# Cached keys and values of a decoder layer: each quad of DMAs split between SyncE's and GpSimd's queues

## What is computed

```python
# fox heads: pages of 128 keys, 8 pages for each of 8 sequences
k_all = concat([cache_fox_k[page_table], ka]); v_all = concat([cache_fox_v[page_table], va])
s = q @ k_all.T * scale + (cum_q - cum_k)        # cum: running sum of log-forget values
oa = softmax(s masked causally) @ v_all
# dilated heads: windows (128, step 1), (512, step 4), (2048, step 16) over a cache of 1024 keys
s = q @ kx[idx].T * scale + bias[distance bucket]
ob = sum over the three patterns of softmax(s) @ vx[idx], weighted by their log-sum-exp
heads = concat([oa, ob]); x = x + gate * (heads @ w_out)
```

## Time and profile before

| | |
|---|---|
| runs | 2654.03 us median of 3 (2649.22 to 2661.18) |
| profiled execution | 2655.89 us; its span from the first to the last instruction 2654.2 us |
| TensorE products / VectorE / ScalarE / GpSimd busy | 94% / 43% / 32% / 2% of the span |
| mean granted TensorE clock | 0.967 |
| DMA | 613.6 MB moved; SyncE's queue ("hardware_dynamic") 603.8 MB, GpSimd's ("software_dynamic") 7.9 MB |
| chain of work that ended last | TensorE 86%, DMA 7%, VectorE 2%, SyncE's issuing 2% |

### The profile page before, as it was taken

The page is one execution under the profiler, slowest core; times in us unless marked ns, Lnnn a source line. Parts: engine busy times, 40 slices in busy tenths (PEclk is TensorE's granted clock), DMA queues, the critical chain, the costliest instruction groups (busy, mean ns, idle before and its releaser), DMA issues.

```text
span 2654.2 us, 50741 instructions
## 1 busy us (share of the span) xinstructions
PE 2487.4 (94%) x20807; PEld 2302.4 (87%) x20807; DVE 1150.1 (43%) x1726; ACT 852.7 (32%) x1060; POOL 44.3 (2%) x92
## 2 busy tenths in 40 slices
PE   5789999999999999899998867798999999999999
PEld 2589999999999999899996334597999999999999
DVE  0433444343443345666641112355444444454444
ACT  1423232333232334534431112335333333333332
POOL 0040000000000000000000000000000000000000
PEclk8799999999999999999998878898999999999999
DMA  9687777677777744344558999853454544454444
GB/s 373 259 318 296 275 309 285 263 280 301 286 282 280 303 162 164 125 158 153 181 198 311 346 347 397 330 173 125 160 172 160 171 160 164 161 169 171 158 160 160
DMA packets 105445, 613.63 MB, mean 231 GB/s; under 512 B 16008, under 2 KB 16288, under 8 KB 55648
## 3 DMA queue, kind: packets, MB, share of 16 engines
q1 hardware_dynamic: 101728, 603.81, 62.1%
q0 software_dynamic: 3584, 7.88, 1.0%
HBM read 604.36 MB, written 7.28 MB: 230 GB/s over the span
## 4 chain that ended last, share of the span: by engine, by line
PE 86%; DMA 7%; DVE 2%; SPq 2%; issue 1%; ACT 1%; ACTq 0%; DVEq 0%
PE banks L592 26%; PE banks L591 26%; PE banks L593 25%; PE banks L619 4%; DMA adax<-in_w_ada_dram 3%; SPq L468 1%; PE banks L886 1%; DMA kv_h<-in_vpool_dram 1%; PE banks L843 1%; DMA kv_raw<-in_wink_dram 1%; DMA kv_z<-in_wink_dram 1%; DVE w_lo L1151 1%; SPq L459 1%; PE banks L705 1%; PE banks L532 1%
## 5 line engine op out<-in xcount | busy, mean ns | idle before, releaser
L591 PE MATMUL banks<-h_hi,w_hi 128*128 128x288 f32 x3792 | 1125.5, 297 | 35.0 <-DVE h_lo L1183 19.2
L592 PE MATMUL banks<-h_lo,w_hi 128*128 128x288 f32 x3792 | 1124.0, 296 | 0.0
L593 PE MATMUL banks<-h_hi,w_lo 128*128 128x288 f32 x3792 | 1122.5, 296 | 0.0
L1151 DVE TENSOR_TENSOR w_lo<-raw,w_hi 128x1024 fp32r<-128x1024 f32 (+2 forms) x666 | 763.6, 1188 | 476.4 <-ACT w_hi L923 469.7
L923 ACT ACTIVATE w_hi<-raw 128x1024 fp32r<-128x1024 f32 (+2 forms) x666 | 671.4, 1031 | 710.0 <-PE banks L593 563.4
L591 PEld LDWEIGHTS banks<-h_hi,w_hi 128*128 128x128 f32 x3792 | 718.1, 189 | 47.6 <-issue 41.4
L592 PEld LDWEIGHTS banks<-h_lo,w_hi 128*128 128x128 f32 x3792 | 718.2, 189 | 0.8
L593 PEld LDWEIGHTS banks<-h_hi,w_lo 128*128 128x128 f32 x3792 | 717.5, 189 | 0.0
L591 PE MATMUL banks<-g_hi,w_hi 128*128 128x288 f32 x1376 | 407.9, 296 | 0.0
L592 PE MATMUL banks<-g_lo,w_hi 128*128 128x288 f32 x1376 | 406.8, 296 | 0.0
L593 PE MATMUL banks<-g_hi,w_lo 128*128 128x288 f32 x1376 | 406.6, 296 | 0.0
(11 more groups left out here) (189 smaller groups left out, 1082.3 us busy)
## 6 DMA issues: line engine op xcount, KB each, us to landing
raw<-in_w_dram SPq DMA_DIRECT2D x172, 1024.0 KB, 4.9
adaw<-in_w_ada_dram SPq DMA_DIRECT2D x56, 1024.0 KB, 6.9
adaw_b<-in_w_ada_dram SPq DMA_DIRECT2D x56, 1024.0 KB, 11.3
raw<-in_w_dram SPq DMA_DIRECT2D x64, 896.0 KB, 4.6
raw<-in_w_in_dram SPq DMA_DIRECT2D x49, 1024.0 KB, 4.9
adax<-in_w_ada_dram SPq DMA_DIRECT2D x32, 1024.0 KB, 8.6
raw<-in_w_dram SPq DMA_DIRECT2D x32, 960.0 KB, 4.8
raw<-in_w_out_dram SPq DMA_DIRECT2D x16, 1024.0 KB, 5.0
```

Source lines behind the costliest of these rows:

```text
L591: pe.matmul(bank[:, 0:T], hi, m_hi[:, k, :], start=k == 0, stop=False)
L592: pe.matmul(bank[:, 0:T], hi, m_lo[:, k, :], start=False, stop=False)
L593: last = pe.matmul(bank[:, 0:T], lo, m_hi[:, k, :], start=False, stop=k == nk - 1)
L1151: dve.tensor_tensor(w_lo[:, r, a:b], raw[:, r, a:b], w_hi[:, r, a:b].bitcast(F32), ALU.subtract).then_inc(S["lo_ready"], 1)
```

## The change

The loop's body becomes a function that issues a part `js` of a quad's four transfers on a given engine, with its waits, its page numbers and a semaphore of its own kind (`kv` or `kw`). SyncE issues sequences 0 and 1 of each quad, GpSimd sequences 2 and 3. GpSimd does so after its last store of line 513; the eight toe loads stand in its order between quads 29 and 30. TensorE waits for both kinds, 32 counts each. The waits for free buffers are the same on both queues.

```diff
+        def half_quad(eng, m, js, mark):
+            kind = 0 if m < quad0[1] else 1
+            n = KIND[kind]["n"]
+            g, v, p = (m - quad0[kind]) // (2 * n), (m - quad0[kind]) // n % 2, (m - quad0[kind]) % n
+            if m == 0:
+                eng.wait_ge(S["head_ready"], 16)
+                eng.wait_ge(S["lf_ready"], 1)
+            if m == 1:
+                eng.wait_ge(S["lo_ready"], 2 * out.n0)
+            if m == 2:
+                eng.wait_ge(S["w_used"], 2 * out.n0)
+            if kind == 1 and (m - 1) % RING == 2:
+                eng.wait_ge(S["heads_stored"], 4 * 16)
+                eng.wait_ge(S["p_s"], HEADS)
+            if kind == 0:
+                pg = [eng.value_load(pages[0:1, (GB * g + j) * PAGES + p:(GB * g + j) * PAGES + p + 1],
+                                     min_val=0, max_val=POOL - 1) for j in js]
+            if m > RING:
+                eng.wait_ge(S["kv_used"], m + 1)
+            for a, j in enumerate(js):
...
+                eng.dma_start(kv(m, j), src.rearrange("a p n -> p (a n)"))\
+                   .then_inc(S[f"{mark}_landed{(m - 1) % RING}" if m else f"{mark}_first_landed"], 16)
...
             sp.wait_ge(S["ld_pages"], 16)
             for m in range(QUADS):
...
+                half_quad(sp, m, (0, 1), "kv")
...
             pool.dma_start(lf_out, lf[:, :]).then_inc(S["heads_stored"], 16)
+            for m in range(quad0[1] - 2):
+                half_quad(pool, m, (2, 3), "kw")
             pool.wait_ge(S["p_s"], HEADS)
             for a in range(0, P, REVS):
                 pool.dma_start(toe[a:a + REVS, :, :],
...
+            for m in range(quad0[1] - 2, QUADS):
+                half_quad(pool, m, (2, 3), "kw")
...
                 def landed(m):
-                    if m:
-                        pe.wait_ge(S[f"kv_landed{(m - 1) % RING}"], 64 * ((m - 1) // RING + 1))
-                    else:
-                        pe.wait_ge(S["kv_first_landed"], 64)
+                    for mark in ("kv", "kw"):
+                        if m:
+                            pe.wait_ge(S[f"{mark}_landed{(m - 1) % RING}"], 32 * ((m - 1) // RING + 1))
+                        else:
+                            pe.wait_ge(S[f"{mark}_first_landed"], 32)
```

More of the change, by code:

```diff
@@ L285, in decoder_layer @@
             hy_ready head_ready lft_sum lft_ready ncum_sum ncum_ready p_s p_max p_exp p_scaled p_v p_vcopy
-            p_t p_tcopy p_o p_high p_low vn_sum vn_ready kv_landed0 kv_landed1 kv_landed2 kv_first_landed
+            p_t p_tcopy p_o p_high p_low vn_sum vn_ready kv_landed0 kv_landed1 kv_landed2 kv_first_landed kw_landed0 kw_landed1 kw_landed2 kw_first_landed
             kv_used qbd_ready nm_ready exp_ready r_ready pt_sum pt_ready os_ready ot_ready oh_ready ol_ready"""
@@ L360, in splits @@
                 split(after_norm[r], j, 0, (q,))
+        def half_quad(eng, m, js, mark):
[18 more added lines that the diff above has]
+            for a, j in enumerate(js):
+                if kind == 0:
+                    src = (vpool if v else kpool)[bass.ds(pg[a], 1), :, :]
+                else:
+                    src = (winv if v else wink)[GB * g + j:GB * g + j + 1, p, :, :]
+                eng.dma_start(kv(m, j), src.rearrange("a p n -> p (a n)"))\
+                   .then_inc(S[f"{mark}_landed{(m - 1) % RING}" if m else f"{mark}_first_landed"], 16)
         def own_rows(c):
@@ L443, in _ @@
             for m in range(QUADS):
[L444 to L465, removed]
-                    else:
-                        src = (winv if v else wink)[GB * g + j:GB * g + j + 1, p, :, :]
-                    sp.dma_start(kv(m, j), src.rearrange("a p n -> p (a n)"))\
-                      .then_inc(S[f"kv_landed{(m - 1) % RING}" if m else "kv_first_landed"], 16)
+                half_quad(sp, m, (0, 1), "kv")
             sp.wait_ge(S["kv_used"], max(m for m in range(QUADS) if (m - 1) % RING == 0) + RING + 1)
```

## The result

The changed kernel takes 2662.13 us in the median of 20 runs (2655.48 to 2668.69) against 2655.36 (2649.22 to 2661.18) for the kernel before: ratio 1.0025, 95% interval 1.0017 to 1.0033. It is 6.8 us slower, where 3 us faster was forecast. That is inside the stated range and inside the 0.5% called "the same", but clear of its interval and of the wrong sign. The profiled execution has a span of 2660.7 us for 2654.2.

The account below looks back on a forecast made before the run. The stage fetching the cached quads was taken as bound by DMA bandwidth, not issuing. Terms: -2.9 - 0.8 - 1.0 + 1.5 + 0.2 = -3.0 us, giving a median of 2651.0 us, range 2642 to 2667.

Parts of the forecast that it names:

- the last paragraph of the change part by part: End of the stage: first w_out tiles compete with GpSimd's half of the last quads; equal bytes, so priced at 0.
- Term 6: Toe loads between GpSimd's halves of quads 29 and 30: their bytes crawl wherever they stand, 0 us.
- Rival C: Toe loads run without company, the other 1.63 MB of quads come later: +4.0 us, 2655; chance 0.07.
- Term 1: First keys, quads 5 to 7: issued when buffers are free, DMA never runs dry from 1424 on; -2.9 us.
- Term 2: First values, quad 14 issued 2.8 us late: gain of what 1476 to 1482 lost, -0.8 us.
- Term 3: Second group: same gain, 0.5 us from 1528 and 0.5 in the refill from 1556; -1.0 us in the sum.
- Term 4: Price of GpSimd's path at the five refills where the queue was empty: 0.3 us each, +1.5 us.
- Term 5: VectorE's 16 SBUF copies in the stage hold up GpSimd's descriptor writes: +0.2 us, at most 2.6.
- The estimate named there: Skill page's port lock: 2.5 us per DMA caught by a VectorE copy, over 40 us if all 16 caught one.
- Rival A: GpSimd's queue drains its half of quads more slowly, 20.9 GB/s per engine: +24.1 us, 2675; chance 0.11.
- Rival B: Two queues also lift the slow ramps after refills: stage gains 7.5 us more, 2642; chance 0.08.

Follow-up runs that it names:

- the control: The changed kernel run once more with no edit, beside the follow-up kernels: 2662.86 us, ratio 1.0037 of the kernel before.
- the alternating kernel: Against the changed kernel, whole quads in turn: even ones on SyncE, odd ones on GpSimd, quads 50 and 51 on SyncE; 2663.18 us, ratio 1.0027.
- the run with both edits: The changed kernel, but quads 50 and 51 wholly on SyncE and the toe loads shared four and four between SyncE and GpSimd: 2653.56 us, ratio 1.0007.

## Why the prediction was wrong

**The step that failed** is the last paragraph of the change part by part: that w_out competing with GpSimd's half of the last quads "moves nothing I can price". I reasoned that both halves carry equal bytes. They do, but SyncE's queue goes on with 2 MB more behind its half, in packets twice as large. In one queue they stood behind the quad; in two they overtake it. Price: 4.2 us in the trace, 4.3 us by taking it away beside the control, and 5.7 us by moving two whole quads. Two edits show it in the runs' times and a third in its trace (there the time, 1.2 us more with an interval from -1 to 6, decides nothing). By itself it outweighs the forecast gain.

**Term 6** put the toe loads at 0, "wherever they stand". Rival C named 4.0 us, for 3.9 in this trace, but the match is partly luck: it had the toe loads without company, and in the changed kernel SyncE's halves took 57.3% of the engines beside them. Whether the missing company costs stays open: with all of it in SyncE's queue it did not (23-33: 62.9 us), in GpSimd's it did (66.9), and the packets differ, 1 KB and 4 KB. By the groups above, 27-33 is 42.9 us in the mean where they stand among GpSimd's quads and 40.2 where they don't: 2.7 us, with 1 to 2 us of scatter in both groups; over 23-33 it is 66.9, with the alternating kernel, and 64.1, without an overlap. But no edit shows it by itself in the runs' times: sharing the toe loads evenly left 23-33 as it was, and the run with both edits gained in all while its 27-33 stayed at 42.4. And the kernel with the quads on GpSimd alone has the cost in one ordered queue, so it is not one of two queues as such. The cost is likely, its path is open, and it is less sure than the tail's.

**Term 1** was -2.9 us and is worth nothing. The lateness was real and is gone, the window's rate rose to 381 GB/s, but quad 7's products end 28.7 us after quad 1's, for 28.4. The first refilled quad comes later (1421.30 to 1431.04 = 9.7 us from issue to use, for 1423.50 to 1432.33 = 8.8), quad 7 arrives 1.2 us sooner by the stage's own clock (1446.36 - 1421.09 for 1449.76 - 1423.29), and its products then ran at the lower clock, 3.41 us for 1.95. **Term 2** with what follows was -0.8 and 7-15 shows -1.7 us; but two kernels with those quads on one queue took 46.7 and 46.8 us there, so this gain isn't shown to be the change's. **Term 3**, -1.0, is drowned in 18-23.

**Term 4**, 0.3 us per refill, is +0.9 at the one where it can be read; small, and the path is not the main cause: in the kernel with both edits 50 of 52 quads still take it for half their bytes, at a ratio of 1.0007. **Term 5**: GpSimd's two issues take 1.04 to 1.19 us from the first refill on, so none was held up for long; 0.2 is not contradicted. (The estimate named there, 16 times 2.48 us, is 39.7 us, not over 40.) **Rival A** is refuted, 25.0 GB/s per engine.

**Rival B**'s sign came and its gain did not. The rate around the first refill, in slices of 1 us, before from 1410 and in the changed kernel from 1408:

```profile
GB/s 344 414 381 303 311 377 430 414 406 135 16 0 0 0 115 311 360 324 352 426 315 352 381 373 401 422 336 377 369 356 414 315 279 377 426 410 422 422 414 406
GB/s 348 291 373 422 410 422 418 381 98 53 0 0 0 0 119 283 397 397 414 406 434 414 426 389 410 410 414 414 401 418 406 414 393 410 406 410 414 410 401 414
```

Within 2 us of its start the changed kernel's refill is at 397 GB/s and stays at 389 or more; before it went up and down between 279 and 426 for longer. Whether the prompt issues or the second queue did this, these runs don't separate. The ramps got faster, and quad 7 ended no sooner.

**What nobody forecast** is the half-clock stretch after quad 18: 7 of 8 traces in which these quads are split or alternate take 26.8 us or more for 18-23, against 24.7 at most for one queue. The kernel that splits only those keys has it too, so it goes with their split, though not always: the kernel with the toe loads shared took 25.0. By which path it comes is open, and by the runs its cost is between nothing and some 4 us.

The terms as measured, 4.2 + 2.7 + 0 to 4 - 1.7, make 5 to 9 us; the runs say 6.8. That is no proof: the terms were picked afterwards, and sections 23-27 and 33-50, -1.1 and -1.5 us, are left out as nothing here accounts for them.

## What to carry to other kernels

A queue is also an order. Before splitting a stream between two queues, list for each queue what stands behind each transfer that somebody waits for: with two queues the engines serve both at once, packet for packet, and a prefetch with large packets takes the larger part of the bandwidth from the transfer that is needed now. If issuing is late but DMA is saturated, as here, a second issuer makes the issues prompt and not the data; split only where the queue is empty behind, and keep the last transfers ahead of a prefetch on the prefetch's own queue.

## What the runs showed of the hardware

- Packet for packet: 181 packets beside 180 in 6 us, 0.65 MB beside 0.49; 158 beside 134 at the tail, where that meant 1.16 MB beside 0.48.
- GpSimd's queue alone moves 410 GB/s with packets of 3.6 KB in the mean (rows of 4 KB), 25.0 GB/s per engine, the same as SyncE's.
- An issue pair on GpSimd, 2 x 512 KB, takes 1.04 to 1.19 us from the first refill on; in the rows shown it takes 1.12 and starts 0.5 us after SyncE's on the same semaphore.
- The same 1 MB of toe loads, runs of 1 KB, is 256 packets of 4 KB in GpSimd's queue and 1024 of 1 KB in SyncE's. With the quads in the same queue and the other queue empty, it holds the engines at some 150 GB/s for 9.5 us in GpSimd's and at some 190 for 7 us in SyncE's.
- After the pause within quad 18, TensorE's clock stayed at its lower level for 2 to 4 us in seven traces, for about 10 in six and for 6 in one, with the same products. The pauses were 2.60 to 3.86 us in the seven and 2.60 to 3.46 in the others, so their length doesn't tell which comes; the fetching of the quads was all that differed.
